# A two-model stack: conv taps in pairs, an attention preparation that does not wait for the conv module, fixed banks, longer chains

## The reference, cut to what matters

```
for l in range(2):                               # first block
    p = rms_norm(x, norm_w[l]) @ w_in[l]         # 2048 x 6668
    qa, ka, va, za, ub, zb, qkv_c, b_c, a_c, zc = split(p)
    qa, ka = rope(rms_norm(qa heads)), rope(rms_norm(ka heads))   # 12 and 4 heads of 64
    oa = sliding_window_sink_attention(qa, ka, va) * silu(za)
    h  = a * sigmoid(gt)                         # ub = a, gt, 512 columns each
    h  = causal_depthwise_conv(h, conv_w) + conv_b                # 31 taps
    ob = (silu(layer_norm(h)) @ pw_w + pw_b) * silu(zb)
    oc = gated_deltanet(qkv_c, b_c, a_c)         # 6 heads of 128, conv of 4 taps, l2 norm,
    oc = rms_norm(oc) * silu(zc)                 #   a triangular solve in chunks of 64
    x = x + concat(oa, ob, oc) @ w_out[l]
for l in range(2):                               # second block
    # 8 heads of differential attention, 4 of gated linear attention (GLA) in both
    # directions, 4 of retention; then a feed-forward of width 5632 with a conv of 3
```

## Time and profile before

| what | us |
|---|---|
| median of three runs | 3596.53 (3594.49 to 3596.84) |
| the profiled execution's own time | 3592.43 |
| its span | 3590.6 |
| PE busy in it | 3448.8 (96%) |
| DVE busy | 2285.3 (64%) |
| ACT busy | 1852.1 (52%) |
| POOL busy | 157.4 (4%) |
| mean granted clock | 0.984 of full |

### The profile page before, as it was taken

One profiled execution on the slowest core, in us unless ns is written; L12 is line 12 of the kernel. 1 busy time (PEld: TensorE's weight loads), 2 busy tenths in 40 slices (PEclk: granted clock), 3 DMA queues, 4 the chain that ended last, 5 costly groups with the idle time before them and its releaser, 6 DMA issues.

```text
span 3590.6 us, 41541 instructions
## 1 busy us (share of the span) xinstructions
PE 3448.8 (96%) x16074; PEld 2776.4 (77%) x16074; DVE 2285.3 (64%) x3130; ACT 1852.1 (52%) x2526; POOL 157.4 (4%) x243
## 2 busy tenths in 40 slices
PE   7989999989999999999999999999999999999998
PEld 5767678767678777788888888887777888888886
DVE  4866565956655666556666666666665566666665
ACT  4464645464645355655454455553565555445444
POOL 3014000023000000000000000000000000000000
PEclk9999999999999999999999999999999999999999
DMA  7434356534356345455655655653444565565564
GB/s 205 135 110 134 100 163 188 145 101 136 99 171 194 98 134 141 138 189 176 198 184 181 197 185 179 193 171 102 149 135 152 188 194 182 187 194 182 186 195 153
DMA packets 399092, 578.51 MB, mean 161 GB/s; under 512 B 25473, under 2 KB 222585, under 8 KB 398256
## 3 DMA queue, kind: packets, MB, share of 16 engines
q1 hardware_dynamic: 392544, 557.93, 50.7%
q0 software_dynamic: 5904, 16.75, 1.6%
q10 hardware_dynamic: 448, 1.18, 0.1%
HBM read 570.78 MB, written 4.98 MB: 160 GB/s over the span
## 4 chain that ended last, share of the span: by engine, by line
PE 82%; DVE 11%; ACT 5%; issue 2%; DMA 1%; DVEq 0%; ACTq 0%; SPq 0%
PE PS L708 79%; DVE WL L1850 3%; PE PS L705 3%; DVE ZA L2041 2%; ACT WH L1314 1%; DVE AR L1990 1%; DMA RAW<-in_w_in 0%; DVE AR L2314 0%; ACT L1577 0%; ACT AR L1659 0%; DVE SM L2247 0%; DVE AR L2245 0%; DMA X<-in_x 0%; ACT AR L1577 0%; ACT AR L1340 0%
## 5 line engine op out<-in xcount | busy, mean ns | idle before, releaser
L1850 DVE TENSOR_TENSOR WL<-RAW,WH 128x1024 fp32r<-128x1024 f32 x1056 | 1292.4, 1229 | 958.1 <-ACT WH L1314 955.4
L1314 ACT ACTIVATE WH<-RAW 128x1024 fp32r<-128x1024 f32 x1056 | 1106.0, 1055 | 977.7 <-PE PS L708 575.7
L708 PE MATMUL PS<-WH,Ah 128*128 128x512 f32 x3520 | 1426.9, 405 | 41.9 <-DVE WL L1850 34.1
L708 PE MATMUL PS<-WL,Ah 128*128 128x512 f32 x3520 | 1383.8, 393 | 0.0
L708 PE MATMUL PS<-WH,Al 128*128 128x512 f32 x3520 | 1382.9, 393 | 0.0
L708 PEld LDWEIGHTS PS<-WH,Ah 128*128 128x128 f32 x3520 | 668.9, 190 | 212.7 <-issue 37.9
L708 PEld LDWEIGHTS PS<-WL,Ah 128*128 128x128 f32 x3520 | 667.5, 190 | 144.3
L708 PEld LDWEIGHTS PS<-WH,Al 128*128 128x128 f32 x3520 | 669.5, 190 | 138.2 <-issue 6.8
L708 PE MATMUL PS<-WH,Zh 128*128 128x512 f32 x704 | 278.4, 395 | 0.6
L708 PE MATMUL PS<-WL,Zh 128*128 128x512 f32 x704 | 274.3, 390 | 0.0
L708 PE MATMUL PS<-WH,Zl 128*128 128x512 f32 x704 | 274.2, 389 | 0.0
(11 more groups left out here) (320 smaller groups left out, 2160.9 us busy)
## 6 DMA issues: line engine op xcount, KB each, us to landing
RAW<-in_w_in SPq DMA_DIRECT2D x368, 512.0 KB, 3.7
RAW<-in_w_up SPq DMA_DIRECT2D x704, 256.0 KB, 3.1
RAW<-in_w_down SPq DMA_DIRECT2D x176, 512.0 KB, 4.0
RAW<-in_w_out SPq DMA_DIRECT2D x64, 512.0 KB, 3.6
RAW<-in_w_o SPq DMA_DIRECT2D x64, 512.0 KB, 3.7
RAW<-in_w_in SPq DMA_DIRECT2D x64, 256.0 KB, 3.1
AR<-in_c POOLq DMA_DIRECT2D x2, 1600.0 KB, 7.4
AR<-bias_scratch POOLq DMA_DIRECT2D x16, 192.0 KB, 4.7
```

Source lines behind the costliest of these rows:

```text
L708: return T.matmul(o, lhs, rhs, start=start, stop=stop, skip_group_check=True)
L1314: act(WH[:, j % NW, 0:n], raw_view(j), ACT.Copy).then_inc(*w_hi())
L1850: tt(WL[:, j % NW, 0:w], raw_view(j), WH[:, j % NW, 0:w].bitcast(F32), SUB).then_inc(*w_lo())
```

## The change

Six edits. (1) mixer_b takes two taps in a place where it took four, so that 60 places carry them instead of 30, and they end in zc.4; mean stands in front of zc.7, var of va.1, and the product with pw_w in front of za0.3 and za0.4. The load of pw_w (PW, in another part of the buffer) moves behind `base` in POOL's queue. (2) mixer_a waits for "qa0" and "qa1" alone; Square, sum and scaling are cut into halves by rows; KS is gone, and eight matmuls of 64 columns of K with the identity put the swapped halves into place in `qt4`. (3) mixer_c starts its norm two places later, and three more yields stand ahead of `ta`: `lt2` now lies in front of qkv3.0, `ta` of zc.2. (4) za0 goes before zb, gv and ga before gqk. (5) In the attention, scores use bank 4, transposes bank 5 and values bank 6, each waiting for the step that empties it. (6) gla: a level every three places; the score matmuls for partitions 0 to 63 go to one bank and those for 64 to 127 to the next, without PE's wait for itself; QE and KE come from one multiplication (QKE), and one predicated copy takes eight blocks.

```diff
-        ("zb", [(3072, 512)]), ("za0", [(1280, 512)])]
-C2CH = [("gqk", [(3072, 512)]), ("gv", [(3584, 512)]), ("ga", [(4608, 32)]), ("gr", [(4096, 512)]),
+        ("za0", [(1280, 512)]), ("zb", [(3072, 512)])]
+C2CH = [("gv", [(3584, 512)]), ("ga", [(4608, 32)]), ("gqk", [(3072, 512)]), ("gr", [(4096, 512)]),
...
-MERGE1 = [("c", (10, 12, 14)), ("b", (6, 8)), ("a", (0, 2, 4))]
+MERGE1 = [("c", (10, 12, 14)), ("a", (0, 2, 4)), ("b", (6, 8))]
...
-                for _ in range(31):
-                    yield
+                for _ in range(63):
+                    yield
+                yield from e.until("qt")
+                T.wait_ge(*a_act.at(m("qc4")))
...
                 yield
+                yield
+                yield
+                yield from e.until("c")
                 yield
                 yield
                 T.wait_ge(*b_dve.at(m("si")))
...
                 yield from e.until("qkv0", "qkv1", "qkv2")
+                yield
+                yield
                 yield
                 for r in range(6):
...
-                for _ in range(12):
+                for _ in range(15):
                     yield
                 T.wait_ge(i_ttm, 64 * (l + 1))
...
-                yield from e.until("qa0", "qa1", "pw")
-                for _ in range(7):
+                yield from e.until("qa0", "qa1")
+                for _ in range(11):
                     yield
                 for c2 in range(5):
-                    T.wait_ge(*a_dve.at(m("ks11")))
-                    if c2 == 0:
-                        T.wait_ge(*b_act.at(m("pb3")))
-                    else:
+                    T.wait_ge(*a_dve.at(m("rope_f1")))
+                    if c2 > 0:
                         T.wait_ge(*a_act.at(m(f"qc{c2 - 1}")))
+                    elif l > 0:
+                        T.wait_ge(*b_act.at(f"{l - 1}.pb3"))
                     for e_ in R2:
                         c = 2 * c2 + e_
                         for t in R2:
-                            src = QK[:, t, 128 * c:128 * c + 128] if c < 8 else KS[:, t, 128 * (c - 8):128 * (c - 8) + 128]
-                            ins = tr(PS[:, 7, 256 * e_ + 128 * t:256 * e_ + 128 * t + 128], src)
+                            o = slice(256 * e_ + 128 * t, 256 * e_ + 128 * t + 128)
+                            if c < 8:
+                                ins = tr(PS[:, 7, o], QK[:, t, 128 * c:128 * c + 128])
+                                continue
+                            for i in R2:
+                                k = 128 * (c - 2) + 64 * (1 - i)
+                                ins = mm(PS[64 * i:64 * i + 64, 7, o], QK[:, t, k:k + 64], ident)
                     ins.then_inc(*a_pe(m(f"qt{c2}")))
                     yield
+                e.flags.add("qt")
...
-                        if i >= 4:
-                            T.wait_ge(*a_dve.at(m(f"gt{i - 4}")))
+                        if i > 0:
+                            T.wait_ge(*a_dve.at(m(f"sb{i - 1}")))
...
+                        if i > 2:
+                            T.wait_ge(*a_act.at(m(f"tc{i - 3}")))
                         for e_ in R2:
                             for k in range(1 + t):
                                 o = W * e_ + 128 * k
-                                ins = tr(PS[:, 4 + (i - 2) % 4, o:o + 128], SBUFS[(i - 2) % 4][:, o:o + 128])
+                                ins = tr(PS[:, 5, o:o + 128], SBUFS[(i - 2) % 4][:, o:o + 128])
...
+                        if i > 3:
+                            T.wait_ge(*a_dve.at(m(f"gt{i - 4}")))
...
+                yield from e.until("gqk")
+
+                def scores(q, k, tiles, names):
+
+                    for i in R2:
+                        at = slice(64 * i, 64 * i + 64)
+                        for c in R2:
+                            for t, (jt, it) in enumerate(tiles):
+                                o = 256 * c + 128 * t
+                                ins = mm(PS[:, names[2] + i, o:o + 128], k[at, c, 128 * jt:128 * jt + 128], q[at, c, 128 * it:128 * it + 128])
+                        ins.then_inc(*g_pe(m(names[i])))
+
                 T.wait_ge(*g_dve.at(m("zn1")))
...
+                T.wait_ge(*s_act.at(f"{l}.gqk.k"))
+                scores(GQ, GK, ((0, 0), (1, 1)), ("dgx", "dg", 4))
                 yield
                 T.wait_ge(c2_in, 16 * (l + 1))
-                for i in range(17):
+                for i in range(26):
                     for d in R2:
-                        n, half = divmod(i - d, 2)
+                        n, k = divmod(i - d, 3)
                         if not 0 <= n < 8:
                             continue
-                        if half == 0:
-                            if n > 0:
-                                T.wait_ge(*g_dve.at(m(f"pa{d}{n - 1}1")))
-                            else:
-                                T.wait_ge(*g_dve.at(m("at1")))
+                        if k == 0:
+                            T.wait_ge(*g_dve.at(m(f"pa{d}{n - 1}" if n else "at")))
...
-                            continue
-                        T.wait_ge(*g_dve.at(m(f"ke{d}{n}")))
-                        qe, ke = two(QE[:, d, :]), two(KE[:, d, :])
-                        for k, (jt, it) in enumerate(((0, 0), (1, 1)) if n < 7 else ((0, 1),) if d == 0 else ((1, 0),)):
-                            for hd in (0, 2, 1, 3):
-                                base, c = 64 * (hd % 2), hd // 2
-                                if hd == 1:
-                                    T.wait_ge(*g_pe.at(m(f"sc{d}{n}{k}x")))
-                                ins = mm(head(5 + 2 * d - k, hd), ke[base:base + 64, c, 128 * jt:128 * jt + 128],
-                                         qe[base:base + 64, c, 128 * it:128 * it + 128])
-                                if hd == 2:
-                                    ins.then_inc(*g_pe(m(f"sc{d}{n}{k}x")))
-                            ins.then_inc(*g_pe(m(f"sc{d}{n}{k}")))
+                        elif k == 2:
+                            T.wait_ge(*g_dve.at(m(f"qk{d}{n}")))
+                            tiles = ((0, 0), (1, 1)) if n < 7 else ((0, 1),) if d == 0 else ((1, 0),)
+                            scores(two(QKE[d][:, 0, :]), two(QKE[d][:, 1, :]), tiles, (f"sc{d}{n}x", f"sc{d}{n}", 4 + 2 * d))
...
                         stt(ACC[:, c, d:256], HB[:, c, 0:256 - d], P(("bcw", l), 4 * j + c), ACC[:, c, d:256],
                             MUL, ADD).then_inc(*b_dve(m(f"t{j}_{c}")))
-                    yield
+                        if c % 2:
+                            yield
+                yield
+                yield
+                yield from e.until("qt")
...
-                yield from e.until("qa0", "qa1", "pw")
-                V.wait_ge(*a_act.at(m("sq")))
-                red(KSS, SQT.rearrange("p t (h d) -> p (t h) d", d=64), AX.X, ADD).then_inc(*a_dve(m("ss")))
-                yield
-                qv = QK.rearrange("p t (h d) -> p (t h) d", d=64)
+                yield from e.until("qa0", "qa1")
+                for t in R2:
+                    V.wait_ge(*a_act.at(m(f"sq{t}")))
+                    red(KSS[:, 16 * t:16 * t + 16], SQT[:, t, :].rearrange("p (h d) -> p h d", d=64), AX.X, ADD).then_inc(*a_dve(m(f"ss{t}")))
+                    yield
+                yield
                 V.wait_ge(*a_act.at(m("rs")))
-                tt(qv, qv, KSS.unsqueeze(2).broadcast_to([128, 32, 64]), MUL).then_inc(*a_dve(m("qn")))
-                yield
...
-                V.wait_ge(*a_dve.at(m("rope_f1")))
-                for t in R2:
-                    src = QK[:, t, 768:1024].rearrange("p (a b d) -> p a b d", b=2, d=64)
-                    dst = KS[:, t, :].rearrange("p (a b d) -> p a b d", b=2, d=64)
-                    for i in R2:
-                        cp(dst[:, :, i, :], src[:, :, 1 - i, :]).then_inc(*a_dve(m(f"ks{t}{i}")))
...
+                    stt(blocks[:, :, t, :], PS[:, 4:6, :].rearrange("p b (c t n) -> p (b c) t n", t=2, n=128)[:, :, t, :], 2.0, idb,
+                        MUL, MUL).then_inc(*g_dve(m("at" if t else "at0")))
...
+                                pred(blocks, mask.unsqueeze(1).unsqueeze(1).broadcast_to([128, 4, 2, 128]),
+                                     pv.rearrange("p b (c t n) -> p (b c) t n", t=2, n=128)).then_inc(*g_dve(m(f"pa{d}{n - 1}")))
...
+                            tt(QKE[d], GQK, EE[:, d, :].unsqueeze(1).broadcast_to([128, 2, 512]), MUL).then_inc(*g_dve(m(f"qk{d}{n}")))
...
-                G.dma_start(PW, a["b_pw_w"][l].rearrange("(c p) n -> p c n", p=128)).then_inc(pw_in, 16)
...
+                G.wait_ge(*c_pe.at(f"{l}.o2"))
+                G.dma_start(PW, a["b_pw_w"][l].rearrange("(c p) n -> p c n", p=128)).then_inc(pw_in, 16)
```

146 lines of the change are left out of this document (77 added, 69 removed).

## The result

The changed kernel takes 3557.5 us (median of four runs, 3556.2 to 3560.6) against 3596.1 before: a ratio of 0.9895, interval 0.9877 to 0.9912. It is 38.6 us faster, where 79 were forecast: the direction is right, the time lies in the range, the gain is a little less than half. The profiled execution takes 3560.6 us, 31.9 less than that of before.

What follows compares the result with a forecast made beforehand. PE's program bounds the kernel, plus places where PE waits for DVE or ACT. Gains of 23.3 us a layer in the first block and 16 in the second, twice 39.3, make 79 us: 3517 us, range 3486 to 3560.

Steps and rivals of the forecast that it cites:

- Term 5: In gla's levels, score calls lose PE's waits for itself and save 1.1 us each: 16 us a layer, bounds 4 and 19.
- two such halves: In gla's score calls, two halves of rows going to two banks at once; a call costs 1.1 us, saves 1.1.
- my first rival: In gla, the halves of the scores don't overlap, a call stays near 1.9 us: 24 us less gain, 3541; chance 0.15.
- Term 1: In qkv1 and qkv2, two taps a place end both waits of PE: 10.3 us a layer gained, lower bound 8.
- Term 2: In qa0 and qa1, later norm and mean cut PE's waits for squares and last tap: 12 us a layer, bounds 8 and 16.
- Term 3: From qkv3 to zc, taps beside POOL run at twice 0.39 us and DVE sets the pace: 2 us a layer lost.
- the second and third rivals: At ta, POOL's chain becomes the bound: 3563, chance 0.10; or the same chain later still, slower, 3610, chance 0.03.
- Term 4: In va, za0 and zb, pw's work moved between waits covers some of them: 3.5 us a layer, between 0 and 7.
- The added work: In the attention, eight small matmuls for the swapped K replace four transposes: 0.5 us more.

Runs made afterwards that it cites:

- the fours: The changed kernel with gla's score instructions ordered four for partitions 0 to 63, four for 64 to 127, and again, instead of eight and eight: ratio to before 0.9868.

## Why the prediction was wrong in size

**Term 5, gla: the step that failed.** I wrote that after, "all sixteen instructions are two such halves" and that a call costs 1.1 us as in ret. It costs 1.64 to 1.7, since PE passed about four instructions of the other half, not eight (its first starts at 1219.439, the first half's at 1218.884); 0.5 us are saved in a call instead of 1.1, and 14 calls a layer miss 8.4. That was my first rival, at 0.15, which had put the call at 1.9. The step leaned on rows with four behind four for a pattern of eight behind eight; I had named that gap and still took 16 out of a range of 4 to 19.

The second part of the term was not named at all: the copy behind the multiplication, 5.5 us lost in dq0.7 and 0.8 in the low clock behind it. I had counted what a place holds and not followed that, in DVE's queue, it stands behind an instruction that waits for ACT, which waits for PE's chunk. -16 + 8.4 + 6.3 leaves -1.3; measured are -1.7 and -3.6. That the two causes are the right ones is shown by the two runs that mend one each (the copy gives back 6.2 and 7.0 us, the fours 4.2 and 5.7 without the swing between gr.1 and gr.3), and by both together, which bring the stretch to the forecast length.

**Term 1, the taps.** Right in mechanism: the waits of 6.9 us fell to 1.5 and the clock is at 1.00. 8.6 and 6.7 us instead of 10.3: PE still waits 0.8 us at most for each burst place, as its own sum (9.0 against 8.2) had it, and layer 1 kept one stretch of half clock (3.4 us) that layer 0 has not.

**Term 2, the norm.** The mechanism is right, the size some 40% too high: -8.7 and -8.0 for a forecast of -12. The run with the norm early shows that the two places are worth something (8 to 14 us in both layers). What stays is 9.8 and 10.5 us, where I had left 6.7 (and 18 - 6.7 is 11.3, not 12): the squares' 4.3 us of waits in layer 0 are near the forecast 5, though the forecast's own figures (32.5 - 21.7 - 8.2) give 2.6, so that this nearness is luck; a wait of 2.2 us for DVE's kb (L2159) with its clock was not named.

**Term 3, LT to TTM.** The mechanism, DVE sets the pace with instructions that POOL slows, is shown by the run without the solve; a tap is slowed by 1.5, not 2. The forecast had 14 us lost there, after has 16.8 and 17.0, so +3.4 and +4.6 for a forecast of +2. POOL's chain did not become the bound, as the second and third rivals had it: its instructions take 0.78 us on average where I had expected 0.9, TTM's loads are issued 65.8 us behind LT, and PE does not wait for TTM; it would, as soon as DVE is relieved (taps in fours).

**Term 4, the attention.** -3.5 were forecast in waits and -2.3 came, mostly in the clock (0.97 to 1.00): the idle time from va to zb is 8.1 us where I had said near 5. The added work was forecast at +0.5, and +1.3 came. I ran nothing that separates the banks from pw's place, so which of them gave the 2.3 stays open.

**The sum.** Of the forecast 79 us, over both layers, gla is short by 26.7, the norm by 7.3, the taps by 5.3, the third term by 4.0 and the attention with the work by 4.0: 47.3. The forecast's terms make 78.6 before rounding; that leaves 31.3 of the traces' 31.9. The parts of the taps and the norm rest on the traces alone; no run removed them.
